# Half of the second key's one-hots of a product-key layer, built by ScalarE instead of VectorE

## The reference

```python
def _peer(h, w_q, sub_keys, u_tab, v_tab):
    q = (h @ w_q).reshape(b, s, PEER_HEADS, 2, PEER_KEY_DIM)
    scores = jnp.einsum('bshpd,hpnd->bshpn', q, sub_keys)
    top_s, top_i = lax.top_k(scores, PEER_TOPK)
...
    expert_idx = jnp.take_along_axis(cand_i, best_pos, axis=-1)
    gates = jax.nn.softmax(best_s.astype(jnp.float32), axis=-1)
...
        act = jax.nn.gelu(jnp.einsum('td,ted->te', xt, u_tab[it]), approximate=False)
        return jnp.einsum('te,ted->td', gt * act, v_tab[it])
```

## Time and profile before

| what | value |
|---|---|
| three runs | 1534.19, 1537.95 (median), 1538.94 us |
| the profiled execution's own time | 1525.29 us |
| its span in the trace | 1523.2 us |
| TensorE busy | 1350.1 us (89% of the span) |
| VectorE busy | 1197.1 us (79%) |
| ScalarE busy | 203.2 us (13%) |
| GpSimd busy | 669.0 us (44%) |
| DMA | 444.22 MB, mean 292 GB/s |

### The profile page before, as it was taken

One profiled execution on the slowest core, in us unless ns is written; L12 is line 12 of the kernel. 1 busy time (PEld: TensorE's weight loads), 2 busy tenths in 40 slices (PEclk: granted clock), 3 DMA queues, 4 the chain that ended last, 5 costly groups with the idle time before them and its releaser, 6 DMA issues.

```text
span 1523.2 us, 18132 instructions
## 1 busy us (share of the span) xinstructions
PE 1350.1 (89%) x6418; PEld 952.0 (63%) x6418; DVE 1197.1 (79%) x2547; ACT 203.2 (13%) x320; POOL 669.0 (44%) x548
## 2 busy tenths in 40 slices
PE   8999989999999999446998898989699999999940
PEld 6787754788888888344444454678588874444410
DVE  5836346778888898899976998999888887666688
ACT  4233010211211022100000101021111110000010
POOL 2243101142433355501656454535365665666672
PEclk9999999999999999755999999999799999999975
DMA  6311423366888899901999898979699999999995
GB/s 231 142 56 56 181 73 116 104 221 222 320 340 338 329 340 415 410 19 37 350 413 413 343 404 285 414 293 362 223 362 401 413 413 413 414 414 413 413 351 209
DMA packets 118281, 444.22 MB, mean 292 GB/s; under 512 B 11568, under 2 KB 24368, under 8 KB 101808
## 3 DMA queue, kind: packets, MB, share of 16 engines
q0 software_dynamic: 73728, 268.47, 46.2%
q1 hardware_dynamic: 43888, 173.56, 29.5%
q10 hardware_dynamic: 576, 1.05, 0.2%
HBM read 440.93 MB, written 2.10 MB: 291 GB/s over the span
## 4 chain that ended last, share of the span: by engine, by line
DVE 35%; PE 29%; DMA 17%; POOL 6%; issue 6%; DVEq 6%; ACT 1%; SPq 0%; ACTq 0%
PE ps L1223 17%; DMA big<-in_peer_v_dram,idx 14%; DVE y L1055 8%; PE ps L1240 7%; DVE big L1034 6%; POOL big L562 3%; POOL big L552 3%; DMA big<-in_peer_u_dram,idx 3%; DVE pool_mem L1125 1%; DVE ohi L1093 1%; DVEq L1106 1%; DVE wr L1074 1%; DVE ohi L1075 1%; PE ps L1382 1%; DVE work L917 1%
## 5 line engine op out<-in xcount | busy, mean ns | idle before, releaser
L552 POOL DMA_INDIRECT big<-in_peer_u_dram,idx x256 | 310.6, 1213 | 582.5 <-DVE dots L1034 468.2
L1034 DVE CUSTOM_DVE_ANT_0 big<-big,xh 128x1024 f32<-128x1024 f32 x256 | 311.5, 1223 | 69.5 <-DMA big<-in_peer_u_dram,idx 46.6
L1055 DVE SCALAR_TENSOR_TENSOR y<-big,wgt,y 128x1024 f32<-128x1024 f32 x256 | 328.1, 1282 | 46.8 <-DMA big<-in_peer_v_dram,idx 42.5
L562 POOL DMA_INDIRECT big<-in_peer_v_dram,idx x256 | 297.4, 1162 | 111.7 <-issue 68.5
L1276 PE MATMUL ps<-big,pool_mem 128*128 128x512 f32 x512 | 225.5, 596 | 0.0
L1223 PE MATMUL ps<-xT,big 128*128 128x256 f32 x1024 | 225.1, 380 | 0.0
L1223 PEld LDWEIGHTS ps<-xT,big 128*128 128x128 f32 x1024 | 193.9, 190 | 26.0
L1276 PEld LDWEIGHTS ps<-big,pool_mem 128*128 128x128 f32 x512 | 97.2, 191 | 119.3 <-issue 119.3
L1276 PE MATMUL ps<-y,pool_mem 128*128 128x512 f32 x256 | 117.8, 612 | 0.8 <-DVEq L1198 0.8
L1223 PE MATMUL ps<-xT 128*128 128x256 f32 x512 | 117.1, 388 | 0.2
L1223 PE MATMUL ps<-xT,y 128*128 128x256 f32 x512 | 117.1, 388 | 0.1
(11 more groups left out here) (222 smaller groups left out, 1356.1 us busy)
## 6 DMA issues: line engine op xcount, KB each, us to landing
big<-u_pairs_dram SPq DMA_DIRECT2D x32, 1024.0 KB, 7.9
big<-v_pairs_dram SPq DMA_DIRECT2D x32, 1024.0 KB, 8.0
y<-u_pairs_dram SPq DMA_DIRECT2D x16, 1024.0 KB, 7.8
xT<-u_pairs_dram SPq DMA_DIRECT2D x16, 1024.0 KB, 7.9
y<-v_pairs_dram SPq DMA_DIRECT2D x16, 1024.0 KB, 8.0
xT<-v_pairs_dram SPq DMA_DIRECT2D x16, 1024.0 KB, 8.0
big<-in_w_in_dram SPq DMA_DIRECT2D x24, 512.0 KB, 5.9
pool_mem<-in_peer_w_q_dram SPq DMA_DIRECT2D x12, 1024.0 KB, 7.5
```

Source lines behind the costliest of these rows:

```text
L552: nc.gpsimd.indirect_dma_start(urow[n % RING], None, peer_u2, bass.IndirectOffsetOnAxis(ap=idx[:, u, e:e + 1], axis=0)).then_inc(s_u[n % R ...
L562: nc.gpsimd.indirect_dma_start(vrow[n % RING], None, peer_v2, bass.IndirectOffsetOnAxis(ap=idx[:, u, e:e + 1], axis=0)).then_inc(s_v[n % R ...
L1034: V.tensor_tensor_reduce(out=urow[n % RING], in0=urow[n % RING], in1=xh[:, u // PH * D:(u // PH + 1) * D], scale=1.0, scalar=0.0, op0=ALU. ...
L1055: V.scalar_tensor_tensor(acc_rows[t], vrow[n % RING], wgt[:, u % 2, e:e + 1], acc_rows[t], ALU.mult, ALU.add).then_inc(s_vadd, 1)
```

## The change

ScalarE makes the one-hots of the last eight tokens of each team. In front of the first `gelu` of the keys it keeps the negated second keys (`minus_key`, in the place of `gated`). For each of eight tokens it writes the absolute value of (counter minus key) over 128 counters, and then in one instruction over all eight, 128x1024, the larger of 0 and (1 minus that). There is one buffer for it, `ohl`, made of `sel`. The job `onehot` for the next team stands right behind ScalarE's copy of a team's bank, which has itself waited for the team's matmuls. VectorE makes the first eight tokens' one-hots alone, in the two halves of `wr` by turns.

```diff
@@ static_jobs, dense_first_half(1) @@
                 add("team", 1, 1, n, by="act")
+                if n + 1 < TEAMS:
+                    jobs.append(("onehot", (1, n + 1), None))
             add("act", r, n, by="act" if r == 0 else "dve")
@@ static_jobs, dense_second_half(0) @@
+        if r == 0:
+            jobs.append(("onehot", (0, 0), None))
...
                 add("team", 1, 0, m, by="act")
+                jobs.append(("onehot", divmod(m + 1, TEAMS), None))
                 if m in between:
                     jobs.append(("gelu", (between[m],), None))
@@ buffers @@
-        ohj3 = [ohj[:, 0], ohj[:, 1]]
...
+        minus_key = gated[:].rearrange("p u k -> p (u k)")
@@ ScalarE @@
+                if kind == "onehot":
+                    s, m = arg
+                    for t in range(8):
+                        c = 16 * m + 8 + t
+                        A.activation(ohl[:, t // 4, :, t % 4], iota[:], ACT.Abs, bias=minus_key[:, c:c + 1])
+                    A.drain()
+                    A.activation(ohl, ohl, ACT.Relu, bias=1.0, scale=-1.0)
+                    A.drain().then_inc(s_ohl, 1)
+                    continue
...
+                    if a == 1:
+                        A.activation(minus_key, selT[:, 1, :], ACT.Copy, scale=-1.0)
+                        A.drain()
@@ VectorE, team_rows_of @@
-                for side in range(2):
-                    e = 2 * g + side
-                    if e >= 3 and e % 2:
-                        dve.wait_ge(s_ohd, (e - 3) // 2 + 1)
-                    elif e >= 3:
-                        b, used_ = BANK[TEAM[(e - 3) // 2]]
-                        dve.wait_ge(full[b], used_ + 1)
-                    V.tensor_tensor(ohj3[e % 3], spread(1, 2 * m + side, NK), both(grid[:], NK), ALU.is_equal)
-                    fence().then_inc(s_oh, 1)
+                V.tensor_tensor(ohj[:, g % 2], spread(1, 2 * m, NK), both(grid[:], NK), ALU.is_equal)
+                fence().then_inc(s_oh, 1)
@@ TensorE, team @@
-                        e = 2 * g + t // 8
-                        if t % 8 == 0:
-                            pe.wait_ge(s_oh, GROUPS + e + 1)
+                        hot = ohj[:, g % 2] if t < 8 else ohl
+                        if t == 0:
+                            pe.wait_ge(s_oh, GROUPS + g + 1)
+                        if t == 8:
+                            pe.wait_ge(s_ohl, g + 1)
...
-                        if t == 7:
-                            last.then_inc(s_ohd, 1)
```

More of the change, by code:

```diff
@@ L209, in static_jobs @@
     for i, (kind, arg, by) in enumerate(jobs):
-        if kind in ("split", "norm", "scale", "gelu", "gates", "expert"):
+        if kind in ("split", "norm", "scale", "gelu", "gates", "expert", "onehot"):
             placed.append((kind, arg, by, None, None))
@@ L366, in layer @@
         sel = sb("sel", [P, 2, 2, PH, TOPK])
-        ohj3.append(sel[:].rearrange("p a b h k -> p (a b h k)").bitcast(f16).rearrange(
-            "p (q n t) -> p q n t", q=2, t=4))
+        ohl = sel[:].rearrange("p a b h k -> p (a b h k)").bitcast(f16).rearrange("p (q n t) -> p q n t", q=2, t=4)
         gated = sb("gated", [P, 2 * PH, TOPK])
+        minus_key = gated[:].rearrange("p u k -> p (u k)")
         dsum = sb("dsum", [P, 2 * PH])
@@ L412, in layer @@
         s_gates, s_selT = sem("gates_ready"), sem("selT_ready")
-        s_oh, s_ohd = sem("onehots_ready"), sem("first_onehots_used")
+        s_oh, s_ohl = sem("onehots_ready"), sem("last_eight_onehots_ready")
         s_act, s_wgtd = sem("dense_gelu_ready"), sem("dense_weights_ready")
@@ L1263, in _ @@
             for kind, arg, by, b, n in JOBS:
-                if kind in ("split", "norm", "scale", "gelu", "gates"):
+                if kind in ("split", "norm", "scale", "gelu", "gates", "onehot"):
                     continue
@@ L1441, in _ @@
                     for t in range(16):
-                        e = 2 * g + t // 8
-                        if t % 8 == 0:
-                            pe.wait_ge(s_oh, GROUPS + e + 1)
+                        hot = ohj[:, g % 2] if t < 8 else ohl
[3 more added lines that the diff above has]
+                            pe.wait_ge(s_ohl, g + 1)
                         for c in range(PIECES):
-                            last = T.matmul(bank[:, t * QUARTER:(t + 1) * QUARTER], ohj3[e % 3][:, t // 4 % 2, :, t % 4],
+                            last = T.matmul(bank[:, t * QUARTER:(t + 1) * QUARTER], hot[:, t // 4 % 2, :, t % 4],
                                             ohi16[:, g % 2, t // 4, c, :, t % 4],
                                             start=(c == 0), stop=(c == PIECES - 1))
-                        if t == 7:
-                            last.then_inc(s_ohd, 1)
                 last.then_inc(full[b], 1)
```

## The result

The changed kernel takes 1516.07 us (median of four runs, 1513.42 to 1519.30); the kernel before, run beside it, 1538.29. The ratio is 0.9878, with a 95% interval of 0.9859 to 0.9898. Two later sets of runs gave 0.9848 (0.9831 to 0.9865) and 0.9855 (0.9833 to 0.9876). That is 22.2, 24.6 and 22.1 us less, where 22.5 was predicted. The profiled execution took 1518.35 us, its span 1516.2.

A forecast was written before the change was run, and what follows sets the result against it. VectorE was taken to pace both engines through the teams; 25.6 us of comparisons, less about 1.5 for waits and 1.5 for gathers, gave -22.5 us, from 1537.95 to 1515.5 us, range 1508.5 to 1531.

The forecast's parts named there:

- VectorE sets the pace between the teams: From 834 to 1125 us VectorE was taken to pace both engines, with TensorE waiting 33.5 us in eight pieces.
- 32 x 0.80 us: VectorE loses one comparison of 0.80 us in each of 32 teams: 25.6 us.
- 1.5 us for the wait for team g-2: Between the teams, VectorE must now wait about 1.5 us for team g-2, leaving 24 of 25.6 us.
- ScalarE, 3.75 us per team, hidden: ScalarE's new one-hots take 3.75 us per team and fit its idle time, 7.42 of 8.01 us.
- three tight places: Spots with little slack for ScalarE's one-hots: two where a unit's exponential and gelu intervene, one with a single expert between teams.
- (c): Between teams (1, 0, 15) and (1, 1, 0), with only one expert, TensorE waits 0.5 us for ScalarE.
- The slower rival's threshold, 8.1 us: Between teams, once ScalarE's one-hots take X = 8.1 us, ScalarE decides and the kernel is slower; up to 1588 us, chance 0.06.
- Which waits of TensorE go: TensorE's waits for VectorE fall from 33.5 to near 20 us; none near 936, longest some 10 at (1, 1, 12).
- 1.5 us to the gathers: Between teams, gathers plus blocks ask 428 GB/s, over the 410 available; 1.5 us taken off the gain.
- The last team: The last team of the second stretch starts 22.4 us earlier, at 1102.3 us instead of 1124.7.
- Nothing comes back later: After the last team all stays but earlier, the gain kept; the rival of losing it there, 1538 us, had chance 0.07.
- 12.7 us between profile and median: The median of whole runs lies 12.7 us above the profiled execution, so 1502.8 us profiled means 1515.5.

The follow-up runs named there:

- e3: Changed kernel with VectorE making its remaining comparison twice over the same buffer: 1531.11 us, ratio 0.9956 to the kernel before.
- g2: Kernel before with a fourth one-hot buffer and without VectorE's two waits for the first half of the team before, both comparisons kept: 1533.37 us, ratio 0.9979.
- e2: Changed kernel without ScalarE's one-hots; TensorE reuses the first eight tokens' one-hots for the last eight: 1511.92 us, ratio 0.9836.
- f1: Changed kernel again, no further edit, run in a set with two kernels that build on it: 1511.84 us, ratio 0.9848.
- g1: Changed kernel a third time, no further edit: 1513.93 us, ratio 0.9855 to the kernel before.
- f2: e7 with the selections of units 9 to 11 also moved later, to rows 126, 142 and 158: 1501.74 us, ratio 0.9772.
- e4: Changed kernel with ScalarE making its one-hots twice: 1554.41 us, ratio 1.0108 to the kernel before.
- e5: Changed kernel with ScalarE making its one-hots three times: 1641.31 us, ratio 1.0762 to the kernel before.
- f3: e7 repeated on one chip with the changed kernel: 1502.63 us, ratio 0.9777 to the kernel before.
- e7: Changed kernel with the normalisation moved from row 160 to 184 and unit 12's selection from row 162 to 171: 1493.40 us, ratio 0.9783.
- e1: Kernel before, unchanged, run for a second profile of it: 1538.58 us, one run.
- e6: Changed kernel with VectorE's normalisation moved from row 160 to 184, past the last team: 1494.94 us, ratio 0.9797.

## Why the prediction was right

By its steps:

- **VectorE sets the pace between the teams.** Shown. With only one comparison more on it (e3) the gain shrinks to 6.8 us, of which g2's missing wait and the cheaper doubled comparison account for 4.2; with ScalarE's work gone (e2) it grows by nothing that two timings of three can tell.
- **32 x 0.80 us.** Right. VectorE's 31 intervals from first to last team took 289.3 us before and take 267.8: 21.5 less, of 24.8 by comparisons. The interval with two rows is 7.02 us, 7.05 predicted.
- **1.5 us for the wait for team g-2.** The size is off and the wait another one. VectorE doesn't wait for TensorE there, it waits 3.3 us for ScalarE's gelu in front of `gated_gelu`, at 990.75 and 1052.55:

```profile
990.75 0.69 DVE L1144 TENSOR_TENSOR pool_mem<-ps,pool_mem 128x512 f32<-128x512 f32 x1 [2.50 <-ACT ps L696]
```

  It leads TensorE by so much that the product of the act job is not there when it asks. 24.8 - 3.3 = 21.5 is just what is measured, and in f1 and g1, where the wait is 2.4 us, 24.8 - 2.4 = 22.4 stands against 289.3 - 266.6 = 22.7. The wait for team g-2 itself is met only with the selections elsewhere (f2), with ScalarE's work doubled or tripled (e4, e5), and for 0.4 us in e2.
- **ScalarE, 3.75 us per team, hidden.** A round in e4 is 3.81 us, of which 2.62 are the Abs, 1.06 the last instruction and 0.13 the drains; 2.5, 1.05 and 0.2 were estimated, 3.75 in all. Of the three tight places only (c), in front of (1, 1, 0), showed a wait, 0.57 us where 0.5 was worked out. In f1 and g1 it is 0.7 and 1.2 us, in f3 2.1.
- **The slower rival's threshold, 8.1 us.** Too high: the loop around X is 1.7 us and not 1.3, and at X = 7.6 us (e4) the kernel was already 1.1% slower. At 3.75 us this didn't matter.
- **Which waits of TensorE go.** The one behind the second selection (936.18 before), as said; the first selection still costs 5.82 us at team (1, 0, 2), which the prediction kept. 9.32 us at (1, 1, 12), 10 said; 20.5 in all, 20 said, but 12.1 and 17.8 in f1 and g1: the waits at the first team and at (1, 0, 2) are 2.57 and 5.82 us here, none in f1, 1.88 and 3.82 in g1. So the match of the sum is in part luck of the execution.
- **1.5 us to the gathers.** Not there: VectorE waits 0.2 us for a row between 848 and 1104 us, though the DMA queues carry 385 GB/s in the first stretch, against 357 before. By this term the prediction was low.
- **The last team.** 268.1 us behind the first by the prediction (1102.3 less 834.2), 270.4 here, 263.2 and 269.0 in the two other profiles of it.
- **Nothing comes back later.** 397.3 us behind the last team, for 398.5. TensorE's stream is the same to 0.1 us: it ended at 1457.4,

```profile
1457.42 1.02 ACT L718 ACTIVATE xh<-ps 128x1024 f32<-128x1024 f32 x1 [7.12 <-PEq L1469]
```

  338.5 us behind the last team, as before (1463.28 less 1124.74). The tail behind it is 58.8 us for 59.9; I had hoped for 1.6 us there and it is 1.1.
- **12.7 us between profile and median.** Taken over as a constant; it turned out to be a difference between sets of runs, with a first team at 834 us in one and 845 to 853 in the others. It did no harm, since it lies ahead of the change, but it was luck that the times to be compared came from sets that were alike. The profiled execution was put at 1502.8 us and took 1518.35, and the last team and TensorE's end, put near 1102 and 1441, came at 1118.9 and 1457.4, since the first team was 14.3 us later. In the set where the kernel before takes 1525 us the change alone was not timed; e7 has there the same ratio as in the slower one (0.9783 and 0.9777), so a like gain is likely, and stays open.

The mis-sized terms (3.3 for 1.5 us, nothing for 1.5) nearly offset each other, which is luck, and what is left of the gain is within the spread of its three timings.

## What to carry to other kernels

An operation that is five times as dear on another engine is still worth moving when the cheap engine sets the pace and the other is idle: work out the loop that the moved step closes (here copy, one-hots, TensorE, 1.7 us + X) and compare it with the shortest interval of the engine that it holds (8.0 us of TensorE), not with the mean (9.2 to 9.4): a loop of 5.5 us fits under that, while one of 9.3, about the mean, made the kernel 1.1% slower. Then see what the waiting engine still waits for: a normalisation and a selection stood ahead of due work, and moving them by some rows gave another 9 us without taking away an instruction. Moving three more selections gave nothing that the time shows; by then TensorE set the pace between the teams. And time a change of 1% beside its own reference, since a profile from elsewhere can be 0.8% off for reasons that have nothing to do with it.

## What the runs showed of the hardware

**TensorE standing for nothing that the trace names.** Ahead of the teams, from 571 to 640 us, the first profile of the kernel before and e1, the same program, differ. Of the first:

```profile
571.00:640.00 69.00, 50.23 (x228) 42.41 (x226) 57.80 (x107) 16.05 (x27) 42.89 (x39) 0.90 1.02 413
```

and of e1:

```profile
571.00:640.00 69.00, 44.50 (x177) 34.74 (x176) 57.38 (x103) 9.15 (x13) 41.99 (x41) 0.82 1.01 403
```

In the first, TensorE gets through 228 matmuls, and its one stand begins at 621 us, a wait of 19.47 us for VectorE; in e1 through 177, and it stands before many of them for nothing that the trace knows of ("issue"):

```profile
580.37 0.38 PE L1223 MATMUL ps<-xT,big 128*128 128x256 f32 x1 [2.43 <-issue]
...
636.51 0.37 PE L1427 MATMUL ps<-ident,sel 128*128 128x128 f32 x1 [3.13 <-issue]
```

The changed kernel has the same, from 540 to 660 us:

```profile
PE ps L1232 <- issue: 11.7, 10, 1.5
PE ps L1433 <- issue: 8.9, 7, 2.2
```

In e1 this eats up nearly all of the 19.47 us that TensorE had to spare, and VectorE then waits for it:

```profile
657.95 0.69 DVE L1125 SCALAR_TENSOR_TENSOR pool_mem<-ps,pool_mem 128x512 f32<-128x512 f32 x1 [10.15 <-PE ps L1435]
```

The same instruction starts at 642.51 us in the first profile, 15.4 us earlier. Every profile of sets 1, 3 and 4 shows these stands and none of set 2 (e5, e6, e7), where the kernel before took 1525.45 us in place of 1536 to 1538. So some 20 us of standing still go with a first team that is 10 to 20 us later, for the same program; they are a property of the place or time of the run. Sets 1 and 2 ran on a chip of the same number, so the chip alone doesn't tell it, unless two chips bear that number.

The DMA engines are full there with and without the stands (share 1.01 and 1.02), but not with the same. From 574 to 592 us, queues by packets, MB and share, in the changed kernel, which stands there, and in the kernel before, which does not; q0 are the gathers, q1 the stream of blocks:

```profile
q0 software_dynamic: 2026, 7.38, 102.6%
```

```profile
q0 software_dynamic: 1315, 4.79, 66.7%
q1 hardware_dynamic: 370, 2.64, 35.4%
```

In that window q0 has 95% or more in all the profiles with stands, and q1 at most 7.1%; without them q0 has 62 to 68% and q1 34 to 39%. TensorE that stands frees no block, so the missing stream can be the effect as well as the cause. That TensorE's instructions come late behind the gathers would fit; it is argued, no run here tested it, and why one set is spared stays open.

**Abs into f16 at a stride of 8 bytes.** The group of the page:

```profile
L602 ACT ACTIVATE sel<-iota,gated 128x128 f16<-128x128 f32 x256 | 83.7, 553 | 0.1
```

256 of them last 553 ns each by their records, but overlap: eight take 2.62 us from the first's start to the last's end, so they start (2.62 - 0.55) / 7 = 0.296 us apart. No cost of the stride is seen in the rate, beside 128x128 packed (0.310 us), and the record's length does not tell the price. The Trainium skill, "ScalarE: Activation LUTs", "What ACT_TABLE_LOAD costs", gives 280 ns + 0.833 N for a bias read per partition and an overlap of 93 ns, an estimate of 0.294 us apart for 128 elements. The trace agrees in the distance, 0.296 us, but not in its parts: the record is 0.553 us long where the page's formula gives 0.387, and the overlap is 0.257 us.
